# One level of Strassen's algorithm in the input projection of a hybrid decoder step

## The reference

```python
def project_in(x, pos, ln_w, w_in, w_gla_a2, b_gla_a):
    h = rms_norm(x, ln_w)                       # (tokens, 1024)
    proj = jnp.einsum('bsd,de->bse', h, w_in)   # w_in: 1024 x 8720
    ...                                         # q, k, v of 24 heads of 64, gates, GLA's q, k, v, decay, mixing gates
def dilated_window_attn_prompt(q, k, v, window, dilation): ...   # 3 groups: (128,1), (512,4), (2048,16)
def dilated_window_attn_sample(q, k, v, kv_buf, window, dilation):
    s = jnp.einsum('bthd,btrhd->bthr', q, kg)   # 8 new tokens against 129 cached keys a group
    ...
def gla_recurrence(q, k, v, log_a, s0, chunk): ...
def merge_out(...): ...                         # gates, three output projections, residual, final norm
```

## Time and profile before

| | us |
|---|---|
| median of 3 runs (2541.37 to 2544.34) | 2543.93 |
| profiled execution | 2544.25 |
| its span, first to last instruction | 2542.5 |
| PE busy, share of the span | 96% |
| DVE, ACT, POOL busy | 50%, 31%, 9% |
| mean granted clock of TensorE | 0.987 |

### The profile page before, as it was taken

How to read it: one execution, slowest core, us unless ns; L and a number is a source line. 1 busy time by engine, 2 the same in 40 slices (tenths; PEclk the granted TensorE clock), 3 DMA queues, 4 the chain that set the end, 5 groups by cost and what they waited for, 6 DMA issues and landing times. The chain is left out here.

```text
span 2542.5 us, 37016 instructions
## 1 busy us (share of the span) xinstructions
PE 2438.7 (96%) x13690; PEld 1978.7 (78%) x13690; DVE 1276.0 (50%) x2963; ACT 798.4 (31%) x1915; POOL 216.6 (9%) x383
## 2 busy tenths in 40 slices
PE   9999999999999999999999999788898987999998
PEld 7888878888888888888877888667777744888887
DVE  5321311211114565666546553677787865665663
ACT  5221222222224322222222221666666533222221
POOL 0000000000000112222233221000000000000000
PEclk9999999999999999999999999999999998999999
DMA  6332222222223457767799778654343369543441
GB/s 190 102 97 82 96 87 89 94 91 89 95 93 123 129 157 227 222 215 227 223 312 290 215 217 246 214 187 143 126 159 125 123 193 346 220 157 119 156 173 67
DMA packets 207137, 413.99 MB, mean 163 GB/s; under 512 B 32000, under 2 KB 52816, under 8 KB 204848
## 3 DMA queue, kind: packets, MB, share of 16 engines
q1 hardware_dynamic: 164928, 290.61, 34.5%
q0 software_dynamic: 29712, 95.06, 13.2%
q10 hardware_dynamic: 12320, 25.96, 2.7%
HBM read 310.48 MB, written 112.86 MB: 167 GB/s over the span
## 5 line engine op out<-in xcount | busy, mean ns | idle before, releaser
L1209 PE MATMUL b_acc<-b_whi,hT_hi 128*128 128x512 f32 x2048 | 799.8, 391 | 8.9 <-DVE b_wlo L926 4.5
L1211 PE MATMUL b_acc<-b_whi,hT_lo 128*128 128x512 f32 x2048 | 797.7, 389 | 0.0
L1210 PE MATMUL b_acc<-b_wlo,hT_hi 128*128 128x512 f32 x2048 | 797.6, 389 | 0.0
L1209 PEld LDWEIGHTS b_acc<-b_whi,hT_hi 128*128 128x128 f32 x2048 | 384.8, 188 | 91.2 <-DVE b_wlo L926 5.3
L1211 PEld LDWEIGHTS b_acc<-b_whi,hT_lo 128*128 128x128 f32 x2048 | 384.8, 188 | 80.3
L1210 PEld LDWEIGHTS b_acc<-b_wlo,hT_hi 128*128 128x128 f32 x2048 | 384.8, 188 | 79.2
L926 DVE SCALAR_TENSOR_TENSOR b_wlo<-b_raw,a_lnw,b_whi 128x512 fp32r<-128x512 f32 x268 | 193.3, 749 | 448.9 <-ACT b_whi L727 448.8
L741 ACT COPY b_stage<-b_acc 128x512 f32<-128x512 f32 (+2 forms) x198 | 115.9, 585 | 726.7 <-PE b_acc L1211 707.9
L758 ACT ACTIVATE c_sm<-c_sm,c_ends 128x256 f32<-128x256 f32 (+1 forms) x384 | 172.4, 451 | 73.7 <-DVE c_ends L1025 73.4
L739 ACT ACTIVATE b_stage<-b_acc 128x512 f32<-128x512 f32 x96 | 57.4, 598 | 425.6 <-PE b_acc L1211 425.6
L727 ACT ACTIVATE b_whi<-b_raw,a_lnw 128x512 fp32r<-128x512 f32 x268 | 186.1, 720 | 7.7 <-DMA b_raw<-in_w_in 4.3
(11 more groups left out here) (315 smaller groups left out, 3033.8 us busy)
## 6 DMA issues: line engine op xcount, KB each, us to landing
b_raw<-in_w_in SPq DMA_DIRECT2D x134, 512.0 KB, 4.3
tm<-b_stage SPq DMA_DIRECT2D x256, 256.0 KB, 2.3
a_x<-tm POOLq DMA_DIRECT2D x192, 256.0 KB, 4.8
b_ck<-in_cache_kv_w POOLq DMA_DIRECT2D x104, 256.0 KB, 4.9
c_qk<-tm SPq DMA_DIRECT2D x96, 256.0 KB, 3.5
f_m<-tm SPq DMA_DIRECT2D x16, 1024.0 KB, 5.8
og<-c_og ACTq DMA_DIRECT2D x48, 264.0 KB, 3.8
c_v<-tm SPq DMA_DIRECT2D x48, 256.0 KB, 4.5
```

The source lines that it names most:

```text
L1209: nc.tensor.matmul(out, stat_hi, mov_hi, start=(k == 0), stop=False)
L1210: nc.tensor.matmul(out, stat_hi, mov_lo, start=False, stop=False)
L1211: return nc.tensor.matmul(out, stat_lo, mov_hi, start=False, stop=(k == KC - 1))
```

## The change

The chunks are taken in pairs (B11 over B21 the one, B12 over B22 the other, split at row 512 of `w_in`), and the tiles in pairs of an even and an odd one (rows A11, A12 and A21, A22 by halves of k). Each pair of chunks and of tiles takes seven block products of 4 steps of k instead of eight. GQK is cut into its two 256-column halves. Eight forms of the normalised input would be A11, A12, A22 and the sums S1 to S4; seven are kept, made by VectorE from the transposes of the odd tile. The sums of weights T1 to T4 are made once, in DRAM, by GpSimd's DMAs: copies, and DMAs that add to their destination (`accum_op`). ScalarE evacuates the first of the seven phases, VectorE adds in the others. The norm's weight is now multiplied into x, as a row broadcast to all partitions. Weights are loaded and split as blocks of 128 x 2048 numbers. Scores are multiplied by GpSimd, the ring of q rows is four. In the late stage eight blocks of values lie where the forms were, and again later.

```diff
-CHUNKS = ((7, 1, 4, 6, 0, 3, GQK, GLR, 9, 10, 11, 12, 13, 14, 15, 8, 2, 5),
-          (8, 2, 5, 7, 1, 4, 6, 0, 3, GQK, GLR, 9, 10, 11, 12, 13, 14, 15))
-W_RING, RAW_RING, STAGES, ACCS, X_RING, CQ_RING, CK_RING, IDLE = 12, 4, 4, 2, 3, 3, 3, (6, 2)
+CHUNKS = ((0, 6), (3, 7), (1, 8), (4, 9), (GQK,), (GLR,), (2, 12), (5, 13), (10, 14), (11, 15))
+HI_RING, LO_RING, ACCS, X_RING, CQ_RING, CK_RING, IDLE = 2, 3, 6, 2, 4, 3, (6, 2)
+AHEAD = 2
+P1, P2, P6, P7, Q4, Q5, Q3 = range(NFORM)
+A_OF = (A11, A12, S2, S3, A22, S1, S4)
+B11, B21, T2, T3, T4, T1, B22 = range(NFORM)
...
+    for phase in range(NFORM):
+        units = [(kind, p) for p in range(NPAIRS if kind == "tm" else 2)]
+        if half == 0 and phase in (P1, P2, Q5, Q3):
+            units.append(("new", 0))
...
+            load_at.setdefault(blocks[b - LO_RING][3] + 1, []).append(b)
+            split_at[blocks[b - 1][2] + 1] = b
+    turn_at = [-1, 0, 1, 2, 3, 5, 6, 7, 8] + [tail + n for n in (11, 13, 15, 17, 24, 26, 28, 30)]
+    stat_at = [max(-1, t - 1) for t in turn_at]
-    item_at = [begin + 3 + m * (NSLOT - 6 - begin - 3) // N_IT for m in range(N_IT)]
+    item_at = [begin + 4 + m * (NSLOT - 8 - begin - 4) // N_IT for m in range(N_IT)]
...
+                def load_w(b):                       # SyncE
+                    if b >= LO_RING:
+                        sp.wait_ge(mm_done, blocks[b - LO_RING][3] + 1)
+                    if phase in T_ROW:
+                        sp.wait_ge(t_in, t_due(turn, phase))
...
+                load_at.setdefault(3, []).append(2)
...
+                def weight_sums(turn):               # GpSimd
+                    pool.dma_start(t3, b22).then_inc(t_in, 16)
+                    pool.dma_start(t2, b11).then_inc(t_in, 16)
+                    pool.wait_ge(t_in, done + 32)
+                    pool.dma_start(t3, b12, accum_op=ALU.add, max_dma_last_dim=2048).then_inc(t_in, 16)
+                    pool.wait_ge(t_in, done + 48)
+                    pool.dma_start(t2, t3, accum_op=ALU.add, max_dma_last_dim=2048).then_inc(t_in, 16)
+                    pool.wait_ge(t_in, done + 64)
+                    pool.dma_start(t4, b21).then_inc(t_in, 16)
+                    pool.dma_start(t1, b11).then_inc(t_in, 16)
+                    pool.wait_ge(t_in, done + 96)
+                    pool.dma_start(t4, t2, accum_op=ALU.add, max_dma_last_dim=2048).then_inc(t_in, 16)
+                    pool.dma_start(t1, b12, accum_op=ALU.add, max_dma_last_dim=2048).then_inc(t_in, 16)
+                    pool.wait_ge(t_in, done + 128)
+                for turn in turns[0:N_TURN]:
+                    if turn.kind != "glr":
+                        if turn.n:
+                            pool.wait_ge(mm_done, turns[turn.n - 1].begin + 1)
+                        weight_sums(turn)
...
+                for m in range(N_IT + AHEAD):
+                    if m < N_IT:
+                        load_item(m)                 # waits for scored >= m - CQ_RING + 1
+                    if m >= AHEAD:
+                        multiply(m - AHEAD)          # nc.gpsimd.tensor_tensor(y, y, ck, ALU.mult)
+                    if copies and item_at[min(m, N_IT - 1)] >= turns[...].end + 6:
+                        copy_window(*copies.pop(0))
...
+                    V.scalar_tensor_tensor(out=x, in0=x, scalar=m[2], in1=lnw_row[0:r, :], op0=ALU.mult, op1=ALU.mult)
+                    elif what == "A1":               # VectorE, an odd tile
+                        link(V.tensor_tensor(a_lo[:, A22, :, c], pt_part(1), hi(A22), ALU.subtract))
+                        link(V.tensor_tensor(raw(S3), hi(A11), pt_part(0), ALU.subtract))
+                        link(V.tensor_tensor(raw(S3), raw(S3), lo(A11), ALU.add))
+                        link(V.scalar_tensor_tensor(out=raw(S2), in0=raw(S3), scalar=-1.0, in1=pt_part(1), ...))
+                        link(V.tensor_tensor(raw(S1), raw(S2), hi(A11), ALU.add))
+                        V.tensor_tensor(raw(S1), raw(S1), lo(A11), ALU.add).then_inc(h_dve, 1)
+                    elif what == "A2":               # one split of S2, S3, S1; B1, B2 do S4 likewise
+                        V.tensor_tensor(a_lo[:, S2:S1 + 1, :, c], a_sum[:, S2:S1 + 1, :, c], a_hi[...], ALU.subtract)
...
+                    if x.phase == P2:
+                        V.tensor_tensor(st_, bank, v_, ALU.add).then_inc(dve_ev, 1)
+                    elif x.phase == P6:
+                        V.tensor_tensor(u_, bank, v_, ALU.add).then_inc(dve_ev, 1)
...
+                    elif x.phase == Q5:
+                        V.tensor_tensor(v_, bank, v_, ALU.subtract).then_inc(dve_ev, 1)
+                        V.tensor_tensor(u_, bank, u_, ALU.subtract).then_inc(dve_ev, 1)
...
+                def load_v(w):                       # late stage, SyncE
+            if held_before(w) is not None:
+                sp.wait_ge(v_used, held_before(w) + 1)
```

More of the change, by code:

```diff
@@ L213, in project @@
[L213 to L228, removed]
@@ L229, in project @@
-    prep_slot = {j: s for s, js in prep_at.items() for j in js}
-    PAIRS = KC * len(heavy) // 2
-    load_after = {}
-    for p in range(2, PAIRS):
-        load_after.setdefault(prep_slot[2 * (p - 2) + 1], []).append(p)
-    NORM = list(range(TPH)) + [NT] + list(range(TPH, NT))
-    tail = turns[len(CHUNKS[0]) - 1].first
-    turn_at = [i - 1 if i <= TPH else tail + i - TPH for i in range(NT + 1)]
-    stat_at = [max(-1, turn_at[i] - 2) for i in range(NT + 1)]
+    slots, turns, blocks = plan_slots()
@@ new lines, in project @@
+    NSLOT, NBLOCK, NCHAIN = len(slots), len(blocks), slots[-1].chain + 1
+    W = plan_projection(nc)
+    begin, last_turn = turns[N_TURN].begin, turns[-1]
+    tail = turns[N_TURN - 1].begin
+    opens = {x.s for x in slots if x.s == min(y.s for y in slots if y.chain == x.chain)}
+    closer = {}
+    for x in slots:
+        closer[x.chain] = x.s
+    first_of = {x.chain: x.s for x in slots if x.s in opens}
+    slot_at = {(x.turn, x.kind, x.phase, x.p): x.s for x in slots}
+    chunk_of = lambda x: turns[x.turn].second if x.phase in (Q5, Q3) else turns[x.turn].first
@@ new lines, in project @@
+    roped = lambda x: turns[x.turn].first < N_ROPED and (x.phase in (P2, Q4) if x.kind == "tm" else x.kind == "new" and x.phase == P2)
+    silu_of = lambda x: turns[x.turn].first in (TM_AZ, TM_GZ) and (
+        x.phase in (P2, Q4) if x.kind == "tm" else x.kind == "new" and x.phase == P2)
+    mixed_of = lambda x: TM_MG <= turns[x.turn].second < N_TM and (
+        x.phase in (Q5, Q3) if x.kind == "tm" else x.kind == "new" and x.phase == Q3)
+    act_of = {"tm": {P1: 1}, "fm": {P1: 1}, "glr": {None: 1}, "new": {P1: 1, P2: 1, Q3: 1, None: 1}}
@@ new lines, in project @@
+    silu_at = {}
+    for x in slots:
+        if silu_of(x):
+            silu_at.setdefault(x.s + 3, []).append(x.s)
+    for s in sorted(silu_at):
+        for n in silu_at[s]:
+            silu_no[n] = len(silu_no) + 1
+    stores_at, store_no, group_end, stored_n = {}, {}, [], [0] * (NPAIRS + 1)
+    group_of = lambda x: NPAIRS if x.kind == "new" else x.p
+    for x in slots:
+        if x.phase in (P2, Q4, Q5, Q3, None) and not (x.kind == "new" and x.phase == Q5):
+            stored_n[group_of(x)] += 1
+            store_no[x.s] = stored_n[group_of(x)]
+            late_by = 3 if x.s in silu_no else 2 if x.s in gate_no else 1
+            stores_at.setdefault(x.s + late_by, []).append(x.s)
+        if x.s == turns[x.turn].end:
+            group_end.append(list(stored_n))
@@ new lines, in one, with rank_one @@
+                    w = width_of(x.block)
+                    rows = k + (KH if x.phase in (P2, Q3) else 0)
+                    return pair(bank[:, 0:w], first, last, hs[:, rows, :], hi[:, 0:w], lo[:, 0:w])
+                def rank_one(x, k):
+                    bank = acc[:, x.chain % ACCS, :]
+                    first, last = k == 0, k == KC - 1
+                    if x.kind == "new":
+                        return nc.tensor.matmul(bank[:, 0:2 * RANK], hs[:, k, :], wr[:, k, :], start=first, stop=last)
+                    f = ((A11, A12), (S1, A22))[x.p][k // KH]
+                    stat = wr2[:, k % KH, :] if x.p and k >= KH else wr[:, k, :]
+                    return pair(bank[0:2 * RANK, :], first, last, stat, a_hi[:, f, k % KH, :], a_lo[:, f, k % KH, :])
```

1038 lines of the change are left out of this document (598 added, 440 removed).

## The result

The changed kernel takes 2584.54 us (median of 4 runs, 2578.43 to 2585.89) against 2542.92 in the same session (2541.37 to 2544.34): a ratio of 1.0159, 95% interval 1.0141 to 1.0177. It is slower by 1.6%; the forecast was 2484, faster by 2.4%, so the direction was wrong, though 2584.5 lies inside the stated 2395 to 2600. The profiled execution took 2578.43 us, its span is 2576.6.

The account below looks back on a forecast made before the run. TensorE was taken as the bound, busy 2438.7 of 2542.5 us. Replacing the projection's 1598.5 us by halves of 852 and 686 gave 2544.25 - 1598.5 + 852 + 686 = 2484 us, range 2395 to 2600.

Parts of the forecast that it names:

- Products removed: Projection on TensorE: 408 fewer products in each half, 816 x 0.2272 = 185.4 us saved.
- The start, 47 us: First tiles: chained VectorE work delays the third phase to near 87 us against 40.4 ideal, 47 us lost, bounds 15 to 65.
- End of the first half, 28 us: Normalising the second half's eight tiles there holds up TensorE's transposes: 28 us lost, bounds 10 to 40.
- Weight sums, 30 us at (2, 12) and hidden elsewhere: DRAM sums hide except after the short rank-16 turn, where pair (2, 12) waits: 30 us lost, bounds 12 and 60.
- The chain of 81 us and the gap of 42: Weight sums if an adding DMA runs at about half a copy's rate: 81 us chain, 42 us gap, total 2496.
- The second half, 686 us: Second half of the projection: TensorE's ideal 656 us, plus 20 for window copies and 10 for full DMA engines elsewhere.
- VectorE "hides" at 62 of 76.4 us a turn: Steady turn: VectorE's adds, splits, rope and score reductions sum to 62 of 76.4 us, hidden behind six banks of products.
- It alone costs nothing: Exclusion between GpSimd multiplications and VectorE's two-SBUF-operand instructions: 7 us more per turn for VectorE, 0.3 per item, no cost alone.
- GpSimd's item, 2.1 us at a landing of 4.4: Second half: landing, issue, key loads and multiplication over three items take 2.1 us an item; the schedule gives 2.88.
- Full DMA engines, 96%: Second half: 202 MB at 320 GB/s take 631 us of TensorE's ideal 656, so DMA is 96% full.
- the 3.6 us item that I had for the window copies: Second half: 28 window copies at 3.6 us an item against 2.88 scheduled, 20 us lost.
- The rival with GpSimd's loop: GpSimd's loop sets the second half's pace: landings 8.3, 3.5 us an item, 789 instead of 686, total 2587; chance 0.14.

Follow-up runs that it names:

- the earlier sums: Changed kernel with VectorE multiplying the scores and the weight sums for pair (2, 12) started one turn earlier: 2493.03 us.
- the order: Changed kernel with three memsets on a private tile replacing each GpSimd multiplication, VectorE waiting as before, score products left out: 2518.13 us.
- a weaker exclusion: Changed kernel with GpSimd multiplying a private tile by itself, VectorE waiting for the DMAs alone, score products left out: 2513.90 us.

## Why the prediction was wrong, step by step

- **Products removed:** right. 5712 full products, 0.389 us for each matmul as before.
- **The start, 47 us:** right. The third phase's first add starts at 91.1 us, its product near 88; 87 was forecast. VectorE was not full before it, though: busy 74 of 92 us.
- **End of the first half, 28 us:** right. From 700 to 849 us TensorE is busy 121.5 of 149, which is 27.6 lost, waiting for the scaled tiles.
- **Weight sums, 30 us at (2, 12) and hidden elsewhere:** right in place and about in size. TensorE waits once, 24.9 us (the first product after the gap, from the timeline), and the granted clock from 440 to 500 us is 0.80:

```profile
480.66 0.76 PE L1473 MATMUL b_acc<-b_whi,a_hi 128*128 128x512 f32 x1 [24.93 <-DVE b_wlo L1151]
```

  With the earlier sums the second half begins 25 us sooner. The chains took 55 to 65 us, 70 were forecast. By line of the kernel, the four adding DMAs of a turn land after 10.0, 10.9, 10.0 and 15.1 us (medians of nine turns), near the 8 to 15 forecast; in the kernel whose sums only copy, the same four land after 6.4, 5.8, 6.6 and 9.1. That is a factor of 1.5 to 1.9, against my one and a half. The Trainium skill (Collectives: The Full Stack, "The bandwidth ceiling") gives half the rate of a copy, for the adding step of a collective. Single landings here come near that, but they do not separate adding from cutting into shorter packets, which only the adding DMAs ask for (`max_dma_last_dim`). The chain of 81 us and the gap of 42 that I had worked out from it did not come. The first half came to 848.4 against 852.
- **The second half, 686 us:** here the forecast failed. It took 783.6. Without any multiplication of scores it takes 703, so 80 of the 98 us too many come with GpSimd's multiplications and 17 from elsewhere.
- **VectorE "hides" at 62 of 76.4 us a turn:** this is the step that failed. As a sum of durations it was not far off: with the 7 us of exclusion that a rival added it was 69, and VectorE was busy 66 (570 us over a half of 8.6 turns). But it was compared with the turn as if VectorE never had to wait. It waited 158 us for GpSimd's products, 18 a turn, and 66 and 18 are more than 76.4. In the second half the rope's first pair took 87 us instead of 28 and the splits 19 us more, since the durations came from a trace in which GpSimd had no multiplication beside them.
- **"It alone costs nothing":** so I priced the exclusion, at 7 us a turn for VectorE and 0.3 for an item. The rule of the Trainium skill (SBUF — State Buffer, "SBUF: two separate sides") was cited rightly, and this trace agrees: 0.98 us for 0.29. Its length was nearly right too, 10 us a turn (87 in the half); its price was not. With the order kept, multiplications on GpSimd cost 83 us, and 10 on VectorE. Left out was what it does in an order: GpSimd's multiplication follows VectorE's reduction by the length of an issue, so it falls on the rope or the split that stands next in VectorE's program, both get longer, and the next reduction is later. That VectorE and GpSimd fall into step so is read from the timeline. Measured is that the two together cost more than a weaker exclusion and the order do apart.
- **GpSimd's item, 2.1 us at a landing of 4.4:** the wrong limit. I counted landing and multiplication over three items, and left out that `load_item(m)`, with three key buffers, waits for reduction m - 3 ahead of multiplication m - 2 in GpSimd's queue. That round is 3.47 us for 8 of 24 items, with a multiplication of 1.3 and not 1.04. Loosening it gave back 36 us of the 83.
- **Full DMA engines, 96%:** did not come. Landings of 5.7 us at a share of 0.78, against the 3.6 us item that I had for the window copies. The forecast's 202 MB were right (254 GB/s over 783 us); in the kernel without multiplications, whose half is 703 us, the share is 0.88.
- **The rival with GpSimd's loop** had the place and the total (789 and 2587 against 783.6 and 2584.5), by another way: landings of 8.3 us, and the exclusion "in the 3.5". That its number came so close is luck: its 3.5 us were for every item, the 3.47 measured are for 8 of 24. For its place, 0.14 was too little.
- **What stays open:** without any multiplication the second half takes 703 us, not 656 or 686. ScalarE waits there for weight blocks (161 us between 850 and 1566) and TensorE for splits (29). In the kernels where VectorE multiplies, loads from ScalarE and later stores did not shorten it. Nor was it measured how the 54 us beyond the parts divide between the heavier exclusion, VectorE's room being used up, and the clock after the gaps.

## What to carry to other kernels

Moving work to an idle engine lost time here, because the two engines met. Before moving an elementwise operation to GpSimd, list VectorE's instructions with two SBUF operands beside it, and write down the round in which the two engines wait for each other, with every issue that stands between. Here VectorE had room for all 148 us of it at a cost of 10. Judge a wait by taking it away: VectorE waited 182 us for a memset at a cost of 17, and 138 us for a multiplication at a cost of 83. And put an engine's waits beside its busy time before saying that it hides. A sum of durations holds only for the neighbours beside which they were measured.

## What the hardware showed that I had not expected

- A GpSimd multiplication of two different 128x512 tensors takes 1.30 us, of one with itself 1.04; a memset of that size 0.53. With the memset beside it no instruction of VectorE got longer (splits 2.28 us, rope 0.29 and 0.29, as without any).
- The exclusion holds for whole instructions, in both directions: 3.44 us for a multiplication that began 10 ns before a split, 1.87 for a rope instruction of 64 columns that takes 0.22 (in the kernel before with GpSimd multiplying). The starts on record do not tell who runs first: that multiplication began before the split and waited, and that rope instruction began 0.47 us before the multiplication and waited too. Additions with an operand in PSUM (0.68 us) and reductions (0.68) kept their length beside it.
- Adding DMAs from DRAM to DRAM land after 10 to 11 us each (15 for the second of two in flight), copies in the same places after 6 to 7 (9). The adding ones were also cut into shorter packets: from 110 to 420 us the software queue moved 23.1 MB in 10144 packets, and 21.0 MB in 4544 with copies.
